# Feed-forward stage of a hybrid decoder step: remainders on VectorE alone, pads, state copies and squares on ScalarE, no arithmetic on Pool

## The reference, cut to what matters

```python
def conv_ffn(x, g, w_up_l, cw, w_down_l, prev):
    u = rmsnorm(x, g) @ w_up_l
    u, new = causal_dwconv(u, prev, cw)
    a, b = jnp.split(u, 2, axis=-1)
    return (jax.nn.silu(a) * b) @ w_down_l, new
...
xp = xp + cross_attn(xp, g_xattn[l], w_xq[l], w_xo[l], mk, mv)
f1, fs1 = conv_ffn(xp, g_ffn[l], w_up[l], ffn_conv_w[l], w_down[l], ...)
xp = xp + f1
```

## Time and profile before

| what | value |
| --- | --- |
| timed runs | 1012.16, 1013.75, 1014.22 us (median 1013.75) |
| profiled execution, first to last instruction | 1012.0 us; no other time is given for it |
| busy, share of the span | PE 92%, DVE 67%, ACT 43%, POOL 45% |
| up loop of layer 1 and of layer 2 | about 287 to 452 us and 772 to 943 us |
| its granted PE clock | 1.00 |

### The profile page before, as it was taken

How to read it: one execution, slowest core, us unless ns; L and a number is a source line. 1 busy time by engine, 2 the same in 40 slices (tenths; PEclk the granted TensorE clock), 3 DMA queues, 4 the chain that set the end, 5 groups by cost and what they waited for, 6 DMA issues and landing times.

```text
span 1012.0 us, 17881 instructions
## 1 busy us (share of the span) xinstructions
PE 932.8 (92%) x6566; PEld 869.0 (86%) x6566; DVE 680.2 (67%) x1260; ACT 435.5 (43%) x728; POOL 460.2 (45%) x701
## 2 busy tenths in 40 slices
PE   6889999998988889889989999999898899898996
PEld 4889988986788888889989998898588888888996
DVE  5567863654459999984455886276345999999533
ACT  4543541434545454444444254143355454453432
POOL 1412310422347777767651231043134777777651
PEclk9989997998689999999999999889868999999999
DMA  8745521566145454445557552139704454453442
GB/s 250 192 114 149 161 72 34 143 183 199 34 118 141 127 159 131 139 143 167 158 147 181 166 166 82 42 98 229 199 1 125 126 163 129 135 158 115 157 146 64
DMA packets 209409, 137.71 MB, mean 136 GB/s; under 512 B 23475, under 2 KB 202203, under 8 KB 209323
## 3 DMA queue, kind: packets, MB, share of 16 engines
q1 hardware_dynamic: 199904, 111.11, 39.2%
q0 software_dynamic: 8288, 22.85, 7.8%
q10 hardware_dynamic: 1131, 2.62, 0.7%
HBM read 131.11 MB, written 5.44 MB: 135 GB/s over the span
## 4 chain that ended last, share of the span: by engine, by line
PE 59%; POOL 16%; ACT 9%; issue 8%; DVE 4%; DMA 1%; POOLq 1%; DVEq 1%; ACTq 0%; SPq 0%
PE banks L1219 12%; PE banks L1220 11%; PE banks L1221 11%; POOL ring_r L875 10%; ACT keysT_r L1116 3%; ACT vals_r L1116 3%; POOL phase L909 3%; PE banks L1397 3%; PE banks L1479 2%; PE banks L1362 2%; PE banks L1319 2%; PE banks L1214 2%; POOL phase L902 1%; PE banks L1447 1%; PE banks L1313 1%
## 5 line engine op out<-in xcount | busy, mean ns | idle before, releaser
L1221 PE MATMUL banks<-mix_r,ring_r 128*128 128x288 f32 x1008 | 302.1, 300 | 0.0
L1894 DVE SCALAR_TENSOR_TENSOR phase<-phase,fpar 128x304 f32<-128x304 f32 x176 | 196.6, 1157 | 4.0 <-issue 0.4
L1221 PEld LDWEIGHTS banks<-mix_r,ring_r 128*128 128x128 f32 x1008 | 195.3, 194 | 0.0
L1219 PE MATMUL banks<-mix_r,ring_r 128*128 128x288 f32 x480 | 151.6, 316 | 9.0 <-issue 6.6
L875 POOL TENSOR_TENSOR ring_r<-ring,keysT_r 128x1024 fp32r<-128x1024 f32 (+2 forms) x36 | 98.9, 2746 | 52.2 <-ACT keysT_r L1116 48.4
L1220 PE MATMUL banks<-XG_r,keysT_r 128*128 128x288 f32 x384 | 115.3, 300 | 0.0
L1219 PEld LDWEIGHTS banks<-mix_r,ring_r 128*128 128x128 f32 x480 | 94.3, 196 | 15.4 <-issue 12.0
L1220 PE MATMUL banks<-XG_r,ring_r 128*128 128x288 f32 x352 | 107.0, 304 | 0.0
L1219 PE MATMUL banks<-mix_r,keysT_r 128*128 128x288 f32 x288 | 89.2, 310 | 18.3 <-POOL ring_r L875 17.0
L1116 ACT CAST ring_r<-ring 128x1024 fp32r<-128x1024 f32 x60 | 62.5, 1046 | 97.9 <-DMA ring<-in_w_in 71.6
L1221 PE MATMUL banks<-phase_r,ring_r 128*128 128x288 f32 x352 | 103.1, 293 | 0.0
(11 more groups left out here) (298 smaller groups left out, 2311.7 us busy)
## 6 DMA issues: line engine op xcount, KB each, us to landing
ring<-in_w_up SPq DMA_DIRECT2D x88, 512.0 KB, 5.1
ring<-in_w_in SPq DMA_DIRECT2D x36, 512.0 KB, 3.9
ring<-in_w_down SPq DMA_DIRECT2D x16, 1024.0 KB, 5.2
ring<-in_w_down SPq DMA_DIRECT2D x8, 768.0 KB, 4.9
rawk<-in_cache_k POOLq DMA_DIRECT2D x32, 128.0 KB, 2.6
vals<-in_cache_v POOLq DMA_DIRECT2D x32, 128.0 KB, 2.4
ring<-in_w_in SPq DMA_DIRECT2D x16, 256.0 KB, 4.0
rawk<-in_cache_mem_k POOLq DMA_DIRECT2D x16, 256.0 KB, 4.7
```

Source lines behind the costliest of these rows:

```text
L1219: mm(out_, hi_w, hi_x, start=start, stop=False)
L1221: return mm(out_, lo_w, hi_x, start=False, stop=stop)
L1894: last = v.scalar_tensor_tensor(out=y[ab][:, 0:304], in0=uab[i % 2][ab][:, w:304 + w], scalar=fpar[:, 3 * l + w, c:c + 1], in1=y[ab][:, 0: ...
```

## The change

Pool keeps its transfers, the pads of the first two steps of each loop, and its arithmetic outside this stage. The second part of the weight remainder goes to VectorE, which subtracts all columns in one instruction; so does the remainder of the gated activation, as a step of its own, `h_rest`, one to two steps behind its `gate`. The activation's remainder at the entry is a fused multiply and subtract on VectorE (`x_rest`), so the plain copy XG is not made there; the squares of the eight tiles move to ScalarE into a buffer `squared`, and VectorE adds them in three instructions at the end. ScalarE copies the new state behind its first tap, and writes the pads from step 2 on. The buffers u grow by four columns, so that prompt and sample state are one strided copy.

```diff
-LO_DVE = {"in": 8, "out": 8, "up": 4, "down": 3}
...
     for i in range(FT):
+        if i >= 2:
+            a("op", "h_rest", i - 2)
...
+    a("op", "h_rest", FT - 2)
     a("op", "convolve", FT - 1)
     a("op", "gate", FT - 1)
     a("op", "round", "down", 2, l)
     a("op", "rest", "down", 2, l)
+    a("op", "h_rest", FT - 1)
...
-        uab = [[ph(306), ph(306)] for _ in range(2)]
+        uab = [[ph(310), ph(310)] for _ in range(2)]
...
+        squared = phase[:, 0:KT_D * N].rearrange("p (k n) -> p k n", k=KT_D)
...
-                elif step == "rest" and args[0] in ("up", "down"):
-                    count, both, lo, hi_part, width, tiles = split_of(*args)
-                    pool.wait_ge(w_hi, count)
-                    cols = slice(LO_DVE[args[0]] * width, tiles * width)
-                    pool.drain()
-                    g_.tensor_tensor(lo[:, cols], both[:, cols], hi_part[:, cols].bitcast(F32),
-                                     ALU.subtract).then_inc(w_lo_pool, 1)
-                elif step == "xo":
...
-                    g_.tensor_tensor(xg_lo[:, k], XG[:, k], xg_hi[k].bitcast(F32), ALU.subtract).then_inc(s["xg_lo"], 1)
-                elif step == "gate":
...
-                    g_.tensor_tensor(hT_lo[:, i], hT[:, i], hT_hi[:, i].bitcast(F32), ALU.subtract).then_inc(s["h_lo"], 1)
-                elif step == "pads":
+                elif step == "pads" and args[0] < 2:
...
-                elif step == "up":
...
-                    g_.tensor_copy(ulast[:, j, g, 0:2], u[:, 256:258])
-                    g_.tensor_copy(ulast[:, j, g, 2:18].rearrange("p (b w) -> p b w", w=2),
-                                   u[:, 258:306].rearrange("p (b x) -> p b x", x=6)[:, :, 4:6]).then_inc(s["u_last"], 1)
...
-                if stage or l:
+                if stage in (1, 3) or (l and stage == 0):
                     ac(XG[:, k], X[:, k], ACT.Identity, scale=par[:, c:c + 1]).then_inc(s["xg_tile"], 1)
...
                     ac(xg_hi[k], X[:, k], ACT.Identity, scale=par[:, c:c + 1]).then_inc(s["xg_hi"], 1)
+                    ac(squared[:, k], X[:, k], ACT.Square).then_inc(s["x_square"], 1)
...
                     ac(yab[i % 2][ab][:, 0:304], uab[i % 2][ab][:, 0:304], ACT.Identity,
                        scale=fpar[:, 3 * l, c:c + 1]).then_inc(s["u_c0"], 1)
+                    nc.scalar.copy(ulast[:, j, g].rearrange("p (k w) -> p k w", w=2),
+                                   u[:, 256:310].rearrange("p (k x) -> p k x", x=6)[:, :, 0:2]).then_inc(s["u_last"], 1)
+                elif step == "pads" and args[0] >= 2:
+                    i = args[0]
+                    act.wait_ge(s["u_conv"], FT * l + i - 1)
+                    for ab in (0, 1):
+                        g, j = divmod(FT * ab + i, UJ)
+                        nc.scalar.copy(uab[i % 2][ab][:, 258:306].rearrange("p (b x) -> p b x", x=6)[:, :, 0:2],
+                                       ust[:, j, g].rearrange("p (b w) -> p b w", w=2))
...
-                pe.wait_ge(w_lo_dve, count)
-                if kind in ("up", "down"):
-                    pe.wait_ge(w_lo_pool, count - SPLIT_PIECES * (l + 1))
+                pe.wait_ge(w_lo, count)
...
+            def x_rest(l, k):
+
+                dve.wait_ge(s["xg_hi"], KT_D * (2 * l + 1) + k + 1)
+                c = par_col(R_FFN, l, k)
+                v.scalar_tensor_tensor(out=xg_lo[:, k], in0=X[:, k], scalar=par[:, c:c + 1], in1=xg_hi[k].bitcast(F32),
+                                       op0=ALU.mult, op1=ALU.subtract).then_inc(s["xg_lo"], 1)
...
-                    cols = slice(0, LO_DVE[args[0]] * width)
+                    cols = slice(0, tiles * width)
...
+                elif step == "h_rest":
+                    i = args[0]
+                    dve.wait_ge(s["h_hi"], FT * l + i + 1)
+                    v.tensor_tensor(hT_lo[:, i], hT[:, i], hT_hi[:, i].bitcast(F32), ALU.subtract).then_inc(s["h_lo"], 1)
...
-                elif step in ("out", "xo", "down"):
+                elif step in ("out", "down"):
                     residual(l, step, args[0])
+                elif step == "xo":
+                    m = args[0]
+                    b_ = put(l, step, m)
+                    v.tensor_tensor(X[:, m], X[:, m], b_[:, 0:N], ALU.add).then_inc(emptied["D"], 1)
+                    if m:
+                        x_rest(l, m - 1)
+                    if m == KT_D - 1:
+                        x_rest(l, m)
+                        dve.wait_ge(s["x_square"], KT_D * (l + 2))
+                        v.tensor_tensor(squared[:, 0:4], squared[:, 0:4], squared[:, 4:8], ALU.add)
+                        drain()
+                        v.tensor_tensor(squared[:, 0:2], squared[:, 0:2], squared[:, 2:4], ALU.add)
+                        drain()
+                        v.tensor_tensor(acc[:], squared[:, 0], squared[:, 1], ALU.add).then_inc(s["sumsq"], 1)
```

More of the change, by code:

```diff
@@ L583, in decoder_kernel @@
         w_hi = sem("w_hi")
-        w_lo_dve = sem("w_lo_dve")
-        w_lo_pool = sem("w_lo_pool")
+        w_lo = sem("w_lo")
         block = ctx.enter_context(nc.Block())
@@ L894, in _ @@
                         wait_emptied(pool, l, "ustate_in", 1)
-                    if i >= 2:
-                        pool.wait_ge(s["u_conv"], FT * l + i - 1)
-                        pool.wait_ge(s["u_c0"], 2 * (FT * l + i - 1))
                     for ab in (0, 1):
                         g, j = divmod(FT * ab + i, UJ)
-                        u = uab[i % 2][ab]
+                        u = uab[i][ab]
                         g_.memset(u[:, 0:2], 0.0)
@@ L1152, in _ @@
                     wait_emptied(act, l, "up", i, ab)
-                    act.wait_ge(s["u_pads"], 2 * FT * l + 2 * i + ab + 1)
-                    if i >= 2:
+                    if i < 2:
+                        act.wait_ge(s["u_pads"], 4 * l + 2 * i + ab + 1)
+                    else:
                         act.wait_ge(s["h_tile"], FT * l + i - 1)
                     c = FT * ab + i
+                    g, j = divmod(c, UJ)
+                    u = uab[i % 2][ab]
                     ac(yab[i % 2][ab][:, 0:304], uab[i % 2][ab][:, 0:304], ACT.Identity,
                        scale=fpar[:, 3 * l, c:c + 1]).then_inc(s["u_c0"], 1)
+                    nc.scalar.copy(ulast[:, j, g].rearrange("p (k w) -> p k w", w=2),
[7 more added lines that the diff above has]
+                                       ust[:, j, g].rearrange("p (b w) -> p b w", w=2))
                 elif step == "convolve":
@@ L1202, in parts_of @@
                 count, _, lo, hi_part, width, _ = split_of(kind, i, l)
-                pe.wait_ge(w_lo_dve, count)
-                if kind in ("up", "down"):
-                    pe.wait_ge(w_lo_pool, count - SPLIT_PIECES * (l + 1))
+                pe.wait_ge(w_lo, count)
                 return [w.rearrange("p (k c) -> p k c", c=width) for w in (hi_part, lo)]
             def xg(l, stage, k):
-                pe.wait_ge(s["xg_tile"], 24 * l + 8 * stage + k + 1 - KT_D)
+                assert stage == 1
+                pe.wait_ge(s["xg_tile"], 2 * KT_D * l + k + 1)
                 return XG[:, k]
@@ L1521, in _ @@
                     cols = slice(P * t, P * t + P) if t < 2 else slice(SEQ, N)
-                    pe.wait_ge(s["xg_tile"], 24 * DEPTH - KT_D + 4 * h + 4)
+                    pe.wait_ge(s["xg_tile"], 2 * KT_D * DEPTH - KT_D + 4 * h + 4)
                     for k in range(4 * h, 4 * h + 4):
```

12 lines of the change are left out of this document (1 added, 11 removed).

## The result

The changed kernel takes 958.22 us (median of 4 runs, 955.25 to 960.14), the kernel before, on the same chip, 1013.3: a ratio of 0.9456, 95% interval 0.9434 to 0.9478. The forecast was 956.3 with a range of 951 to 970, and the measured time lies inside it. Medians here are of fast executions: of the four of experiment 9 one, at 2197.6 us, is in a slow state and is left out.

A forecast was written before the change was run, and what follows sets the result against it. VectorE, held by Pool, was taken to pace the up loop, with PE also waiting at the entries. Gains of 23.4 + 23.2 + 2 x 6.4 = 59.4 us, less 2, gave 57.4 off: 956.3 us from 1013.75, range 951 to 970.

The forecast's parts named there:

- VectorE was held by Pool: Up loop: Pool's remainders slow VectorE's convolution instructions, so 2.67 us of each 7.48 us step is VectorE held.
- The hold of 2.67 us: Up loop, per step: 0.54 + 2.13 us in which Pool's 288-column and 1024-column remainders hold VectorE's convolution.
- VectorE's new step, 6.35, under PE's 6.39: Up loop: VectorE's step falls from 7.48 to 6.35 us (6.27 to 6.56), so PE at 6.39 becomes the limit.
- The first rival: Up loop: VectorE is the next limit, step 6.5 to 7.0 us, 5 to 26 us given back, 961 to 982; chance 0.15.
- The loop sum, 23.4 and 23.2: Up loops of layers 1 and 2: gain in us from steps at PE's 6.39 and most of the first wait.
- The entry, 6.4 each: Entry to each up loop: 12.97 us falls to 6.6 as VectorE hands out tiles sooner; gain 6.4 us per layer.
- The 2 us for late first remainders and handovers: Deduction of 2 us from the 59.4 us gain, for late first weight remainders in the loops and small handovers.
- the total, 57.4: Whole kernel: 59.4 us of gains less 2 us, taken off the profiled span of 1012.0 us.
- The third rival: Up loop: VectorE was not held by Pool; its step becomes 8.94 us and the kernel 1062 us; chance 0.04.

The follow-up runs named there:

- experiment 9: The kernel before, with one edit: VectorE subtracts the whole weight remainder of the up-projection, Pool's half goes; 972.43 us, ratio 0.9595.
- pool_reads: Changed kernel plus a Pool subtraction of 1024 columns in SBUF, awaited by nobody, in 19 steps of each up loop; 1019.33 us, ratio 1.0072.
- pool_writes: Changed kernel plus two Pool memsets of 1024 columns, awaited by nobody, in 19 steps of each up loop; 956.16 us, ratio 0.9439.
- half_on_pool: Changed kernel with Pool again doing the second half of each up-projection weight remainder; 982.26 us, ratio 0.9688.
- after_again: The changed kernel itself, run again without any edit on the same chip as the runs beside it; 957.92 us, ratio 0.9455.
- pads_on_pool: Changed kernel with the up loop's pads and state copies given back to Pool, remainders staying on VectorE; 956.1 us, ratio 0.944.
- late_state: Changed kernel with Pool's four loads of the recurrent state in layer 2 put later, at the convolution state's step; 958.09 us, ratio 0.9452.

## Why the prediction was right, step by step

**VectorE was held by Pool.** This is shown, by pool_reads against pool_writes, and by half_on_pool in the kernel's own work. The hold of 2.67 us was 2.68 in the step of the earlier trace rows (4.71 against 2.03).

**VectorE's new step, 6.35, under PE's 6.39.** It is 6.09, below the lower end of 6.27. Two terms were too large: both remainders were priced by durations, but instructions in a row on VectorE start before the one ahead has ended, so the wide remainder adds 2.21 - 1.27 = 0.94 from start to start (1.01 taken at least) and the activation remainder 0.36 (0.45 to 0.51). That makes up 0.16 of the 0.18; nothing came of the error since PE limits at 6.40. The first rival was closer than it looked all the same: 0.3 us a step.

**The loop sum, 23.4 and 23.2.** What was taken for 20 steps of the loop, 301.21 to 451.13, is 19 steps (to 443.63) and the first 48 matmuls of the down-projection, and 7.50 us is a mean: single steps took 6.9 to 8.1. The sum holds all the same: 156.96 - 134.87 = 22.1 and 1.2 at the down-projection's first 96 matmuls, 23.3; 156.81 - 134.87 = 21.9 and 1.3, 23.2.

**The entry, 6.4 each.** 12.97 - 6.59 and 12.97 - 6.60: 6.4 each. The cause was named rightly, the squares on VectorE. The last remainder ended 1.1 us ahead of PE's need as worked out (272.88 + 0.35 + 21 x 0.133 = 276.0, and 274.35 + 0.52 = 274.9). DVE:

```profile
274.35 0.52 DVE L1549 SCALAR_TENSOR_TENSOR XG_r<-X,par,rawk_r 128x288 fp32r<-128x288 f32 x1 [0.18 <-ACT rawk_r L942]
```

**The 2 us for late first remainders and handovers.** This term was wrong in kind: PE waits nowhere in either loop, and at step 3 no remainder is late. Terms of 59.3 us came true and the span fell by 56.9. The 2.4 us between them are the longer stretch of layer 2, in that execution (239.35 us, 237.48 in after_again of the same kernel); the 0.8 us gained ahead of the first entry and the 0.8 lost in the down-projections cancel. So it is luck that the total, 57.4, came within 0.5 us: a term wrong in kind met a scatter of its size.

**The third rival** would have had VectorE's step grow by what it takes over. It fell by 1.4 us (7.48 to 6.09), and half_on_pool shows why: giving half a remainder away costs 2.05 us held for 1.08 us saved. Of the advice of the Trainium skill in Perfetto Trace Analysis, section Optimizing Scalar/DVE Operations, these traces bear out in the loop the caution on the shared port. Unloading a full VectorE paid only where it went to ScalarE, with the squares at the entry.

**What carried the change.** The parts were forecast as a bundle; the runs divide them. Of 56.9 us the up-projection's wide weight remainder alone brings the loops' share (43.4 of 44.0 us), the squares on ScalarE all but some 2 us of the entries', and pads, state copies and the loop's activation remainder, each undone by itself, nothing that could be measured. The down-projection's wide remainder was not tried by itself.

## What to carry to other kernels

When an engine looks full, compare the same instruction at quiet and at busy moments before counting its load as work: of VectorE's 7.48 us a step 2.67 were waiting, and taking over Pool's work shortened the step. Splitting an element-wise job between VectorE and Pool, both reading SBUF, cost more here than it saved (2.05 us held for 1.08); if Pool keeps such work, let it start inside a long VectorE instruction and be something that nobody waits for soon. Idle time of an engine that waits for another hides its drains, so its room is found by adding a known instruction, not by reading the idle time.

## What the runs showed of the hardware that was not expected

**The hold goes both ways.** In pads_on_pool 38 of the 88 copies of 16 columns, 0.2 us each when free, took 2.2 us on POOL. The one shown began 0.13 us after VectorE's remainder; that one took its usual time. DVE, and POOL:

```profile
345.61 2.31 DVE L1625 TENSOR_TENSOR ring_r<-ring,keysT_r 128x2048 fp32r<-128x2048 f32 x1
345.74 2.23 POOL L888 COPY phase<-ust 128x16 f32<-128x16 f32 x1
```

**A VectorE instruction with one input can be held beside a memset.** The memsets of pool_writes left the convolution (two inputs in SBUF) alone. Beside the one of late_state a VectorE instruction with one input, 288 columns in 0.31 us when free, took 1.13 us more, and it ended 0.31 us behind the memset; it is one instance. The Trainium skill, SBUF — State Buffer, section Who interferes with whom, says that in a two-port performance mode, which such an instruction can enter, VectorE contends with GpSimd. The trace agrees; that this instruction ran in that mode no row says. In the changed kernel the same instruction took 1.55 us while Pool issued loads. DVE, and POOL:

```profile
494.86 1.55 DVE L1558 TENSOR_SCALAR sqr<-sqr 128x288 f32<-128x288 f32 x1
495.72 0.54 POOL L782 DMA_DIRECT2D phase<-in_state_conv  x1
496.23 1.50 POOL L783 MEMSET phase<- 128x1536 f32 x1
```

It ends at 496.41, and if its own work is the last 0.31 us, this began before that memset did. This speaks for the issuing as what held it there; no run tries that by itself, so it stays open.
